# Compression columns ordered block by block, 272 in place of 290, and one transposed block of compressed probabilities for both query halves

## What is computed

```
sub = kv[:, :n_half * CMP_STRIDE].reshape(b, n_half, CMP_STRIDE, 2, NSA_KV_HEADS, HEAD_DIM)
pos = phi_pos.reshape(2, n_sub, CMP_STRIDE, HEAD_DIM)
w1 = phi_w1.reshape(2, n_sub, CMP_STRIDE, HEAD_DIM, HEAD_DIM)
for m in range(n_sub):
    part = jnp.einsum('bnscgd,csdh->bncgh', sub + pos[:, m]..., w1[:, m])
    part = part[:, m:m + n_cmp]
    hid = part if hid is None else hid + part
out = jnp.einsum('bncgh,che->bncge', jax.nn.silu(hid), phi_w2)
...
p_cmp = masked_softmax(s, kc_end[None, :] <= q_pos[:, None])
o_cmp = jnp.einsum('bgrtn,bgnd->bgrtd', p_cmp, vc)
return gates[..., 0:1] * o_cmp + gates[..., 1:2] * o_sel + gates[..., 2:3] * o_win
```

## Time and profile before

| | |
|---|---|
| median of 3 runs | 1113.35 us |
| span of the profiled execution | 1110.9 us |
| median less span (start and end of the execution; the page has no own time for the profiled one) | 2.4 us |
| TensorE busy | 1100.0 us, 99% |
| VectorE, ScalarE busy | 606.3 us, 419.5 us |
| mean granted TensorE clock | 0.996 |
| DMA, mean | 182 GB/s |

### The profile page before, as it was taken

The page is one execution under the profiler, slowest core; times in us unless marked ns, Lnnn a source line. Parts: engine busy times, 40 slices in busy tenths (PEclk is TensorE's granted clock), DMA queues, the critical chain, the costliest instruction groups (busy, mean ns, idle before and its releaser), DMA issues.

```text
span 1110.9 us, 19312 instructions
## 1 busy us (share of the span) xinstructions
PE 1100.0 (99%) x8020; PEld 1077.8 (97%) x8020; DVE 606.3 (55%) x884; ACT 419.5 (38%) x566; POOL 66.8 (6%) x121
## 2 busy tenths in 40 slices
PE   9999999999999999999999999999999999999996
...
PEclk9999999999999999999999999999999999999998
...
GB/s 297 196 189 201 228 279 189 179 152 152 168 147 173 83 113 110 114 171 295 288 277 306 257 149 171 171 171 171 171 167 153 168 145 144 147 242 146 148 150 95
DMA packets 64081, 202.03 MB, mean 182 GB/s; under 512 B 6647, under 2 KB 35607, under 8 KB 45831
## 3 DMA queue, kind: packets, MB, share of 16 engines
...
## 4 chain that ended last, share of the span: by engine, by line
PE 99%; DVE 1%; issue 0%; DVEq 0%
PE bank L1327 27%; PE bank L1328 27%; PE bank L1329 27%; PE bank L1679 1%; PE bank L1360 1%; PE bank L1455 1%; PE bank L1450 1%; PE bank L1429 1%; PE bank L1428 1%; PE bank L1427 1%; PE bank L1594 1%; PE bank L1517 0%; PE bank L1452 0%; PE bank L1685 0%; PE bank L1345 0%; PE bank L1454 0%
## 5 line engine op out<-in xcount | busy, mean ns | idle before, releaser
L536 ACT ACTIVATE w_hi<-raw 128x2048 fp32r<-128x2048 f32 x140 | 268.1, 1915 | 572.2 <-PE bank L1329 479.9
L1327 PE MATMUL bank<-h_hi,w_hi 128*128 128x320 f32 x1536 | 479.7, 312 | 0.0
L1329 PE MATMUL bank<-h_hi,w_lo 128*128 128x320 f32 x1536 | 474.6, 309 | 0.0
L1328 PE MATMUL bank<-h_lo,w_hi 128*128 128x320 f32 x1536 | 474.5, 309 | 0.0
L814 DVE TENSOR_TENSOR w_lo<-raw,w_hi 128x2048 fp32r<-128x2048 f32 x140 | 325.2, 2323 | 186.4 <-ACT w_hi L536 186.2
L1327 PEld LDWEIGHTS bank<-h_hi,w_hi 128*128 128x128 f32 x1536 | 288.4, 188 | 3.9 <-issue 3.5
L1328 PEld LDWEIGHTS bank<-h_lo,w_hi 128*128 128x128 f32 x1536 | 288.5, 188 | 0.4
L1329 PEld LDWEIGHTS bank<-h_hi,w_lo 128*128 128x128 f32 x1536 | 288.4, 188 | 0.0
L1328 PE MATMUL bank<-oz_lo,w_hi 128*128 128x320 f32 x256 | 78.9, 308 | 0.0
L1329 PE MATMUL bank<-oz_hi,w_lo 128*128 128x320 f32 x256 | 78.8, 308 | 0.0
L1327 PE MATMUL bank<-oz_hi,w_hi 128*128 128x320 f32 x256 | 78.8, 308 | 0.0
...
## 6 DMA issues: line engine op xcount, KB each, us to landing
...
```

The source lines that it names most:

```text
L536: nc.scalar.activation(w_hi[:, u], raw[:, u], ACT.Copy).then_inc(hi_ready[u], 1)
L1327: nc.tensor.matmul(out[:, 0:n], w_hi[:, u, kb, :], hi[:, kb, :], start=(kb == first), stop=False)
L1328: nc.tensor.matmul(out[:, 0:n], w_hi[:, u, kb, :], lo[:, kb, :], start=False, stop=False)
L1329: mm = nc.tensor.matmul(out[:, 0:n], w_lo[:, u, kb, :], hi[:, kb, :], start=False, stop=(kb == last))
```

## The change

The columns of `c_hi` and `c_lo_pos` are ordered by block and then by row (block n of all 18 rows side by side), with the two embedding columns of m = 0 ahead of block 0 and a second copy of them behind block 15. So m = 0 multiplies columns 0 to 271 and m = 1 columns 20 to 291: 15 blocks of 18, and 2. `c_lo` of the keys keeps its layout and its 296 columns, and its products go to banks of their own (`S2`, `OB`), which `hidden_in(0)` adds. The copies into the new order are made for each of the two pages apart, and the embeddings apart from them. In the heads, `p_c` packs both query halves into one block of 128 columns (32 for each), one transpose turns it, and two matmuls of 128 columns use `vc_g` (values in rows 0 to 14) and `vc_h` (rows 32 to 46). Line numbers in the listings of the changed kernel's order are those of that kernel.

```diff
+CMP_USED = 2 * SEQS * CMP_STRIDE + CMP_LEN // CMP_STRIDE
+CMP_COLS = 2 * SEQS * N_CMP + CMP_LEN // CMP_STRIDE
...
-        p_c = at("p_c", [P, 2, P], f32, Z_ + 15 * 4 * TOK)
+        p_c = at("p_c", [P, 4, 32], f32, Z_ + 15 * 4 * TOK)
+        vc_h = at("vc_h", [P, P], f32, Z_ + 15 * 4 * TOK + 4 * P)
...
+        def block_columns(t, q0, q1, half, g):
+            columns = t[:, positions(half), 2:2 + CMP_STRIDE * 2 * SEQS].rearrange("p s (g n q) -> p g q s n", g=PAGES, q=2 * SEQS)
+            return columns[:, g, q0:q1]
...
+        def pos_columns(t, half, m):
+            return t[:, positions(half), m * CMP_USED:m * CMP_USED + 2]
...
-            def cmp_high(c, q0, q1, half=None):
-                src, dst = raw_blocks(c, q0, q1, half), high_blocks(q0, q1, half)
-                nc.scalar.activation(dst, src, ACT.Copy).then_inc(c_hi_rdy, 1)
+            def cmp_high(c, q0, q1, half=None, pos=True):
+                if pos:
+                    for m in range(2):
+                        nc.scalar.activation(pos_columns(c_hi, half, m), raw_pos(c, half), ACT.Copy)
+                nc.scalar.activation(block_columns(c_hi, q0, q1, half, 0), raw_blocks(c, q0, q1, half, 0), ACT.Copy)
+                nc.scalar.activation(block_columns(c_hi, q0, q1, half, 1), raw_blocks(c, q0, q1, half, 1), ACT.Copy).then_inc(c_hi_rdy, 1)
...
-                nc.scalar.activation(pt_ab[:, 1, :], P1[:], ACT.Copy).then_inc(pt_win_copied, 1)
+                nc.scalar.activation(pt_ab[:, 1, 0:384], P1[:, 0:384], ACT.Copy).then_inc(pt_win_copied, 1)
...
-            def cmp_low(c, q0, q1, count, half=None):
-                src, high, dst = raw_blocks(c, q0, q1, half), high_blocks(q0, q1, half), low_blocks(c, q0, q1, half)
+            def cmp_low(c, q0, q1, count, half=None, pos=True):
                 dve.wait_ge(c_hi_rdy, count)
-                nc.vector.tensor_tensor(dst, src, high.bitcast(f32), ALU.subtract).then_inc(c_lo_rdy, 1)
+                if pos:
+                    for m in range(2 if c else 1):
+                        nc.vector.tensor_tensor(low_pos(c, half, m), raw_pos(c, half), pos_columns(c_hi, half, m).bitcast(f32), ALU.subtract)
+                    if c == 0:
+                        rest = [t[:, 2 * SEQS, 0:PAGE].rearrange("p (s n) -> p s n", s=CMP_STRIDE)[:, :, 2:] for t in (c_lo, cmp_t[:, 0])]
+                        nc.vector.tensor_copy(*rest)
+                for g in range(PAGES):
+                    src, high, dst = raw_blocks(c, q0, q1, half, g), block_columns(c_hi, q0, q1, half, g), low_blocks(c, q0, q1, half, g)
+                    ins = nc.vector.tensor_tensor(dst, src, high.bitcast(f32), ALU.subtract)
+                ins.then_inc(c_lo_rdy, 1)
 
             with dve.Fori(0, J_PHI - J_Q - 2) as k:
...
             def hidden_in(c):
                 first, second = ((S0, P0), (S1, P1))[c]
                 rows = hx[:, c, 0:270].rearrange("p (q n) -> p q n", n=N_CMP)
-                ch.link(nc.vector.tensor_copy(st[:, c:c + 1], first[:, 288:289]))
-                ch.link(nc.vector.tensor_scalar_add(rows, first[:, 0:288].rearrange("p (q n) -> p q n", n=CMP_STRIDE)[:, :, 0:N_CMP], st[:, c:c + 1]))
-                ch.link(nc.vector.tensor_copy(st[:, c:c + 1], second[:, 289:290]))
-                nc.vector.scalar_tensor_tensor(rows, second[:, 0:288].rearrange("p (q n) -> p q n", n=CMP_STRIDE)[:, :, 1:CMP_STRIDE],
-                                               st[:, c:c + 1], rows, ALU.add, ALU.add).then_inc(hid_x, 1)
+
+                def by_row(bk, first):
+                    return bk[:, first:first + 270].rearrange("p (n q) -> p q n", q=2 * SEQS)
+
+                ch.link(nc.vector.tensor_copy(st[:, c:c + 1], first[:, 0:1]))
+                ch.link(nc.vector.tensor_scalar_add(rows, by_row(first, 2), st[:, c:c + 1]))
+                ch.link(nc.vector.tensor_copy(st[:, c:c + 1], second[:, 271:272]))
+                ins = nc.vector.scalar_tensor_tensor(rows, by_row(second, 0), st[:, c:c + 1], rows, ALU.add, ALU.add)
+                if c == 0:
+                    for m, low in enumerate((S2, OB)):
+                        ch.link(ins)
+                        ch.link(nc.vector.tensor_copy(st[:, c:c + 1], low[:, 288 + m:289 + m]))
+                        blocks = low[:, 0:288].rearrange("p (q n) -> p q n", n=CMP_STRIDE)[:, :, m:m + N_CMP]
+                        ins = nc.vector.scalar_tensor_tensor(rows, blocks, st[:, c:c + 1], rows, ALU.add, ALU.add)
+                ins.then_inc(hid_x, 1)
...
                 if i % REP == 0:
-                    nc.vector.tensor_copy(vc_g[0:N_CMP, :], S1[0:N_CMP, 384:512]).then_inc(vc_rdy, 1)
+                    nc.vector.tensor_copy(vc_g[0:N_CMP, :], S1[0:N_CMP, 384:512])
+                    nc.vector.tensor_copy(vc_h[32:32 + N_CMP, :], S1[0:N_CMP, 384:512]).then_inc(vc_rdy, 1)
...
+            pe.wait_ge(v_rows_rdy, 2 + 4)
             low = c_lo[:].rearrange("p q (g s n) -> p s (q g) n", g=PAGES, s=CMP_STRIDE)
             for k in range(4):
                 part(0, J_PHI + k, h_hi, h_lo, TOK, ALL)
                 c, m = k // 2, k % 2
                 out = ((S0, P0), (S1, P1))[c][m]
                 pe.wait_ge(lo_ready[1], J_PHI + k + 2)
+                columns = slice(0, CMP_COLS) if m == 0 else slice(2 * SEQS + 2, 2 * SEQS + 2 + CMP_COLS)
                 for s in range(CMP_STRIDE):
                     if m == 0 and s % 8 == 0:
                         pe.wait_ge(c_lo_rdy, 2 * c + s // 8 + 1 if c else 2)
-                    nc.tensor.matmul(out[:, 0:used], w_hi[:, 1, s, :], c_hi[:, s, 0:used], start=(s == 0), stop=False, skip_group_check=True)
+                    nc.tensor.matmul(out[:, 0:CMP_COLS], w_hi[:, 1, s, :], c_hi[:, s, columns], start=(s == 0), stop=False)
                     if c == 0:
-                        nc.tensor.matmul(out[:, 0:runs * n].rearrange("p (q n) -> p q n", n=n), w_hi[:, 1, s, :], low[:, s, 0:runs], start=False, stop=False, skip_group_check=True)
+                        nc.tensor.matmul((S2, OB)[m][:, 0:runs * n].rearrange("p (q n) -> p q n", n=n), w_hi[:, 1, s, :], low[:, s, 0:runs],
+                                         start=(s == 0), stop=(s == CMP_STRIDE - 1))
                     else:
-                        nc.tensor.matmul(out[:, 0:used], w_hi[:, 1, s, :], c_lo_pos[:, s, 0:used], start=False, stop=False, skip_group_check=True)
-                    mm = nc.tensor.matmul(out[:, 0:used], w_lo[:, 1, s, :], c_hi[:, s, 0:used], start=False, stop=(s == CMP_STRIDE - 1), skip_group_check=True)
+                        nc.tensor.matmul(out[:, 0:CMP_COLS], w_hi[:, 1, s, :], c_lo_pos[:, s, columns], start=False, stop=False)
+                    mm = nc.tensor.matmul(out[:, 0:CMP_COLS], w_lo[:, 1, s, :], c_hi[:, s, columns], start=False, stop=(s == CMP_STRIDE - 1))
...
-                    nc.tensor.transpose(bk[:, 384:512], p_c[:, n, :], ident[:])
+                    if n == 0:
+                        nc.tensor.transpose(bk[:, 384:512], p_c[:].rearrange("p q n -> p (q n)"), ident[:])
...
-                pt_sel, pt_win, pt_c = pt_ab[:, 0, :], pt_ab[:, 1, :], pt_ab[:, :, 384:512]
+                pt_sel, pt_win, pt_c = pt_ab[:, 0, :], pt_ab[:, 1, :], pt_ab[:, 0, 384:512]
...
-                nc.tensor.matmul(OB[:, 0:SEQ].rearrange("p (q c) -> p q c", q=2), vc_g[:], pt_c, start=False, stop=True)
+                for q, vc in enumerate((vc_g, vc_h)):
+                    nc.tensor.matmul(OB[:, q * P:(q + 1) * P], vc[:], pt_c, start=False, stop=(q == 1))```

TensorE, the first compression tile (keys, m = 0; the rows ahead of it end a query tile), before and then changed:

```order
L1329 MATMUL bank<-h_hi,w_lo 128x320
L1450 MATMUL bank<-c_hi,w_hi 128x290 [waits c_lo_rdy,lo_ready1]
L1452 MATMUL bank<-c_lo,w_hi 128x296
L1455 MATMUL bank<-c_hi,w_lo 128x290
L1450 MATMUL bank<-c_hi,w_hi 128x290
L1452 MATMUL bank<-c_lo,w_hi 128x296
L1455 MATMUL bank<-c_hi,w_lo 128x290
```

More of the change, by code:

```diff
@@ L1046, in prompt_softmax @@
                 ch.link(nc.vector.tensor_tensor(p_c[:, 1, 0:N_CMP], S0[:, 384 + N_CMP:384 + 2 * N_CMP], mask_cmp[:, 1, 0:N_CMP], ALU.add))
-                nc.vector.reduce_max(nmx[:, 0:2], p_c[:, :, 0:N_CMP], AX, negate=True).then_inc(max_rdy, 1)
+                nc.vector.reduce_max(nmx[:, 0:2], p_c[:, 0:2, 0:N_CMP], AX, negate=True).then_inc(max_rdy, 1)
                 ch.link(nc.vector.scalar_tensor_tensor(p_sel[:], dist[:, 128:512], slope, S0[:, N_CMP:384 + N_CMP], ALU.mult, ALU.add))
@@ L1112, in _ @@
             nc.vector.memset(vc_g[:], 0.0).then_inc(pc_zero, 1)
+            nc.vector.memset(vc_h[:], 0.0).then_inc(pc_zero, 1)
             nc.vector.memset(p_c[:], 0.0).then_inc(pc_zero, 1)
-            dve.wait_ge(pc_zero, 2)
+            dve.wait_ge(pc_zero, 3)
             prompt_softmax(0)
@@ L1436, in _ @@
                     part(u, k + J_Q, h_hi, h_lo, TOK, ALL)
-            used = 2 * SEQS * CMP_STRIDE + CMP_LEN // CMP_STRIDE
             n = PAGE // CMP_STRIDE
-            runs = -(-used // n)
```

(5 more changed lines are left out.)

36 lines of the change are left out of this document (19 added, 17 removed).

## The result

The changed kernel takes 1119.43 us (median of 5 runs, 1117.85 to 1119.73) against 1113.18 for the kernel before beside it: ratio 1.0054, interval 1.0043 to 1.0065. It is slower by 0.54%, where 1111.3 us and a chance of 0.06 for slower were on record. A second measurement later gave 1119.41 against 1113.21, ratio 1.0051 (1.0035 to 1.0068).

A forecast was written before the change was run, and what follows sets the result against it. The prediction took TensorE to bound the kernel, busy 1100.0 of 1110.9 us with 99% of the chain. Compression -1.28 and heads -0.78 us sum to -2.06, taking the median from 1113.35 to 1111.3 us; range 1110.4 to 1112.6.

The forecast's parts named there:

- no penalty on a read: VectorE's copy of the own rows, 399 ns for 256 elements read 64 bytes apart, was taken as about full rate.
- +0.3 us for each half: ScalarE's copies into c_hi: each extra instruction adds about 0.1 us, so each half takes 0.3 us longer.
- about 0.15 us more each: VectorE's low parts: each was to take about 0.15 us longer with the new copies.
- The reserves of 0.8 and 1.9 us: Slack left after the change: ScalarE's idle before its weight copy, 0.8 us; VectorE's lead at position 8 of k = 2, 1.9.
- The rival that came true: Strided copies run at half speed and TensorE waits, together +4.7 - 2.1 = +2.6 us, 1116.0 us; chance 0.06.
- No DMA is added or moved: Transfers: the value tile's load waits for the same w_lo, going out 0.5 us later, a whole tile ahead of use.
- Compression products: TensorE's 160 matmuls of 290 columns become 272 wide, saving 8 ns each: -1.28 us, between 0 and 2.3.
- The bank switch of the low products: The keys' low products write another bank than their neighbours, 32 times: taken as 0, at most 0.8 us either way.
- Heads: One transpose fewer in each of 8 heads, -0.86 us, and two smaller value products, +0.08: sum -0.78 us.
- The sum: Compression and heads together: -1.28 - 0.78 = -2.06 us, the median going from 1113.35 to 1111.3 us.
- `hidden_in`: For the keys, one more copy and sum for each of two banks: 1.41 us becomes 2.8, no wait at k = 3.

The follow-up runs named there:

- e4: The kernel before with 27 copies and subtractions of 512 elements, side by side or at various steps, added behind its end; one run, 1134.14 us.
- e2: The changed kernel with the copies into c_hi and c_lo_pos in runs of 8, same instructions, counts and sizes; 1111.12 us, ratio 0.9979.
- e11: The changed kernel with SyncE issuing the last page's loads ahead of the weight tile that waits for the late w_lo; 1115.33 us, ratio 1.0015.
- e12: The changed kernel itself, not edited, measured and profiled again; 1119.41 us (4 runs), its profiled execution 1119.49 us.
- e1: The kernel before with the heads' part of the change alone, the compression as before; 1112.92 us against 1113.42, ratio 0.9992.
- e7: The changed kernel with its 272 columns in another order, only blocks 0 and 15 (288 of 2304 elements) still read in steps; 1111.16 us, ratio 0.9979.

## Why the prediction was wrong

- **The step that failed: "The nearest row is VectorE's copy of the own rows, read 64 bytes apart ... so no penalty on a read."** It took a plain copy at the rate of a subtraction for one at full rate. No row of before showed that copy side by side; e4 did (427 ns for 512) and turned the same 399 ns into evidence for the penalty. From that reading came "+0.3 us for each half" of ScalarE, which was +2.4 with its small copies (254.39 to 259.06, 4.67 us, against 2.25), and VectorE's "about 0.15 us more each", which was +2.1 (259.09 to 263.85, 4.76 us, against 2.69). Without the steps, in e2, the halves take 2.56 and 2.80 us: +0.3 and +0.1, as worked out for more instructions. The reserves of 0.8 and 1.9 us were right as well (e2 has 0.81 and 263.73 - 261.70 = 2.0) and far too small for the steps.
- **The rival that came true** had 0.06 and 1116.0 us. Its first place in the front was sized well, 0.7 computed against 0.75. At k = 2 it had 1.3 and 2.0 against 1.57 and 1.39. At k = 3 it had 0.7 against none: TensorE itself comes there 3 us later. It missed the largest part. "No DMA is added or moved" was true and not enough: SyncE's weight tile waits for the `w_lo` that VectorE delivered late, and the page that ScalarE needs next is queued behind it (2.58 us, e11). And it had no term for the clock behind so long a wait (1.4 us, e12).
- **Compression products**, -1.28 us from 8 ns each: e2's four tiles take 6.53 + 6.60 + 6.04 + 5.98 = 25.15 us against 6.89 + 6.88 + 6.45 + 6.45 = 26.67 before, 1.5 us less, 9.5 ns each. Right in mechanism, a little small. The bank switch of the low products cost nothing visible: k = 0 and k = 1 save 0.36 and 0.28 us for 32 products each.
- **Heads**, -0.78 us: right, -0.77 in e1's trace (its times alone, -0.5, leave it open). In the profile of the changed kernel one transpose of `p_c` is left in head 0, and the two value products of 128 columns take 359.00 - 358.55 = 0.45 us against 0.43 in the earlier trace rows, as worked out.
- **The sum** of both, -2.06 us: e2 gives -2.3, e7 -2.3 (1111.16 against 1113.47). The forecast of 1111.3 us is, within 0.2, the time of the change without its stepped copies.
- **`hidden_in`** with two more banks, 2.8 us: as forecast, 273.04 to 275.94, and no wait at k = 3. The reads 18 elements apart cost nothing (0.50 us).
- **The account**: e2's 1111.1, the waits 0.75 + 2.58 + 1.57 + 1.39 = 6.3, the longer distances behind them 0.4, and e12's 1.6 for the lower clock and the longer wait give 1119.4, as measured. That it closes so well is partly luck: in the start of the program TensorE waits 0 to 1.6 us for `x_t` from one execution to the next.

What stays open: why the clock falls in some executions and not in others with the same wait was not tried.
